# Modulation rows in bursts inside the HGRN scan's slots, and projections ahead of two waits for normed outputs

## The reference, cut to what matters

```
m_lat = (silu(c) @ ada_w[l] + ada_b[l]);  m_ctx = silu(c_ctx) @ ada_w[l] + ada_b[l]
sh1, sc1, g1, sh2, sc2, g2 = split(m, 6)
u = layer_norm(x) * (1 + sc1) + sh1
h = u @ w_in[l]                                  # columns for three mixers
y = concat[rwkv7 scan, differential attention, hgrn2 scan] @ w_out[l]
x = layer_norm(ALPHA * x + g1 * y)
x = layer_norm(ALPHA * x + g2 * peer_ffn(layer_norm(x) * (1 + sc2) + sh2))
```

## Time and profile before

| | us |
|---|---|
| median of 3 runs | 6001.18 (5999.1 to 6006.35) |
| profiled execution | 6002.42 |
| its span, first to last instruction | 6000.6 |
| PE busy | 5152.3 (86%) |
| DVE busy | 3722.8 (62%) |

### The profile page before, as it was taken

How to read it: one execution, slowest core, us unless ns; L and a number is a source line. 1 busy time by engine, 2 the same in 40 slices (tenths; PEclk the granted TensorE clock), 3 DMA queues, 4 the chain that set the end, 5 groups by cost and what they waited for, 6 DMA issues and landing times.

```text
span 6000.6 us, 63022 instructions
## 1 busy us (share of the span) xinstructions
PE 5152.3 (86%) x22127; PEld 3419.4 (57%) x22127; DVE 3722.8 (62%) x8344; ACT 1465.9 (24%) x3650; POOL 1470.7 (25%) x1540
## 2 busy tenths in 40 slices
PE   8899887888776899999999589978798657999997
PEld 3588553667643455555555368845475545666664
DVE  1544371756966797877665455434465786786565
ACT  1111031322566221112111211002222283121111
POOL 0000000000126555545553000000000055344552
PEclk9899988589887999999999789989758757999998
DMA  6000001004358999999997100000002258999996
GB/s 227 21 12 8 21 5 56 1 22 151 124 195 326 366 415 411 400 399 409 401 409 302 62 11 8 8 25 15 35 1 85 105 207 346 416 420 419 416 416 266
DMA packets 294042, 1191.31 MB, mean 199 GB/s; under 512 B 24800, under 2 KB 106976, under 8 KB 208224
## 3 DMA queue, kind: packets, MB, share of 16 engines
q0 software_dynamic: 92160, 671.13, 27.3%
q1 hardware_dynamic: 195808, 460.83, 20.8%
q10 hardware_dynamic: 5760, 55.33, 2.3%
HBM read 1135.81 MB, written 51.38 MB: 198 GB/s over the span
## 4 chain that ended last, share of the span: by engine, by line
PE 62%; DVE 19%; DMA 10%; ACT 4%; issue 2%; POOL 2%; ACTq 0%; DVEq 0%; SPq 0%; POOLq 0%
PE psum L537 62%; DMA arena<-in_ut 6%; DVE arena L1476 3%; DMA arena<-gate_blocks 2%; DVE arena L1631 1%; DVE arena L1822 1%; DVE x_tokens L1476 1%; DVE arena L1897 1%; DMA arena<-in_uv,arena 1%; DVE arena L1485 1%; DMA x_tokens<-in_uv,arena 1%; DVE arena L1629 1%; DVE u_features L1482 1%; DVE y_features L1726 1%; ACT y_features L1169 1%
## 5 line engine op out<-in xcount | busy, mean ns | idle before, releaser
L537 PE MATMUL psum<-arena 128*128 128x64 f32 (+4 forms) x8128 | 1439.3, 352 | 31.2 <-DVE arena L1822 24.2
L537 PE MATMUL psum<-u_features,weight_ring 128*128 128x256 f32 (+2 forms) x4672 | 1351.6, 441 | 31.2 <-ACT arena L1198 17.5
L537 PEld LDWEIGHTS psum<-arena 128*128 128x128 f32 (+1 forms) x8128 | 1032.5, 212 | 399.3 <-issue 309.5
L537 PEld LDWEIGHTS psum<-u_features,weight_ring 128*128 128x128 f32 x4672 | 883.6, 193 | 401.1 <-issue 193.5
L1454 POOL TENSOR_TENSOR arena<-consts 128x1 f32<-128x1 f32 x640 | 335.2, 524 | 1231.3 <-DVE y_features L1726 1098.8
L537 PE MATMUL psum<-u_features,arena 128*128 128x384 f32 (+1 forms) x2048 | 581.5, 438 | 41.3 <-DMA arena<-in_ut 37.2
L537 PE MATMUL psum<-weight_ring,consts 128*128 128x512 f32 x1280 | 570.4, 592 | 2.3 <-DVE consts L1713 1.9
L537 PE MATMUL psum<-arena,y_features 128*128 128x128 f32 (+1 forms) x1632 | 375.3, 387 | 192.1 <-ACT y_features L1171 87.3
L537 PEld LDWEIGHTS psum<-u_features,arena 128*128 128x128 f32 x2048 | 392.3, 192 | 253.7 <-issue 56.3
L1455 POOL DMA_INDIRECT arena<-in_uv,arena x350 | 486.8, 1391 | 99.3 <-POOL arena L1454 94.0
L1087 ACT ACTIVATE arena<-psum 128x512 f32<-128x512 f32 (+5 forms) x388 | 237.6, 612 | 1095.3 <-PE psum L537 864.0
(11 more groups left out here) (208 smaller groups left out, 5361.4 us busy)
## 6 DMA issues: line engine op xcount, KB each, us to landing
weight_ring<-in_ws SPq DMA_DIRECT2D x242, 512.0 KB, 3.6
weight_ring<-in_ut SPq DMA_DIRECT2D x128, 512.0 KB, 10.6
weight_ring<-in_uv SPq DMA_DIRECT2D x128, 512.0 KB, 13.0
arena<-in_ut SPq DMA_DIRECT2D x128, 512.0 KB, 16.2
arena<-in_uv SPq DMA_DIRECT2D x128, 512.0 KB, 10.5
gate_blocks<-arena ACTq DMA_DIRECT2D x20, 2048.0 KB, 7.6
arena<-gate_blocks SPq DMA_DIRECT2D x32, 768.0 KB, 17.8
arena<-gate_blocks SPq DMA_DIRECT2D x32, 512.0 KB, 27.8
```

Of the source, the lines that this page charges most:

```text
L537: return pe.matmul(o, w, x, start=first, stop=last, skip_group_check=True)
```

## The change

Only four chunks of 512 columns (the first 2048, `sh1` and `sc1` of layer 0) stay at the start (`HEAD_ADA`). The other 4096 columns of layer 0 and the first 2048 of layer 1 are computed in layer 0's HGRN scan as 24 chunks of 256 columns, the remaining 4096 of layer 1 in its own scan as 16. `scan_ada` puts a chunk's eight matmuls in front of the level in the slots (n, d) = (1,0), (2,1), (4,0), (5,1), in place of the warm-up multiplication there. `ada_columns` turns the four rows of an iteration in the first slot of the next. ScalarE's copies stand at the iteration's end and behind the next one's first placing. VectorE adds the bias for the later columns in the fifth iteration. The `ada` events leave the opening's list; the rest of that list stays as it was.

The second part: PE projects the last two query/key pieces and the values right after `rwkv g` (which moves to other PSUM banks), and turns `rwkv y` behind the second rotation. After attention it projects four of the six HGRN pieces before it turns `attn y`, and the other two after. ScalarE's copies follow the same order.

```diff
@@ -59,7 +59,9 @@
 ADA, RW, AQK, AV, HF, HT, WO, WQ = 48, 7, 8, 4, 6, 4, 8, 16
-PIECES = [(2 * ADA if l == 0 else 0) + RW + AQK + AV + HF + HT + WO // 2 + WQ * len(QUERIED[l]) for l in range(DEPTH)]
+HEAD_ADA, OWN_ADA = 4, 16
+SCAN_ADA = [24, 16]
+PIECES = [(4 * HEAD_ADA if l == 0 else 0) + 2 * SCAN_ADA[l] + RW + AQK + AV + HF + HT + WO // 2 + WQ * len(QUERIED[l]) for l in range(DEPTH)]
@@ -293,6 +295,9 @@
+        ADA_ROWS = [XT[0:2, 256 * j:256 * (j + 1)] for j in range(4)]
+        ADA_AT, ADA_BANK = ((1, 0), (2, 1), (4, 0), (5, 1)), (3, 4, 0, 7)
+
         def hset(i, d):
@@ -572,6 +572,29 @@
+            def scan_ada(l, i, n, d):
+
+                if (n, d) not in ADA_AT or 4 * i >= SCAN_ADA[l]:
+                    return False
+                j = ADA_AT.index((n, d))
+                if i and n % 2:
+                    pe.wait_ge(*at("scan ada kept", l, 4 * i + j - 4))
+                for k in range(KB):
+                    w = piece_now() if k % 4 else piece_ready()
+                    ins = mm(bank(ADA_BANK[j], 0, 256)[0:2, :], CC[:, 2 * k:2 * k + 2],
+                             w[:, k % 4 * 256:(k % 4 + 1) * 256], k == 0, k == KB - 1)
+                    if k % 4 == 3:
+                        piece_done(ins, *(("scan ada rows", l, 4 * i + j) if k == KB - 1 else ()))
+                return True
+
+            def ada_columns(l, i):
+
+                if 0 <= 4 * i < SCAN_ADA[l]:
+                    pe.wait_ge(*at("scan ada kept", l, 4 * i + 3))
+                    for j in range(8):
+                        ins = mm(bank(0, 2 * j, 2 * j + 2), ADA_ROWS[j // 2][:, j % 2 * P:(j % 2 + 1) * P], ident[0:2, 0:2])
+                    done(ins, "scan ada turned", l, i)
+
             def project(l, what, count, first=0):
@@ -748,8 +771,8 @@
                     pe.wait_ge(*at("cond silu"))
-                    for c in range(ADA // 4 + 1):
-                        if c < ADA // 4:
+                    for c in range(HEAD_ADA + 1):
+                        if c < HEAD_ADA:
                             if c >= 2:
@@ -898,26 +921,26 @@
                 for t in range(NT):
-                    ins = mm(PS[:, t * 256:(t + 1) * 256], lo_[64:128, t * P:(t + 1) * P], SW[64:128, 0:256])
+                    ins = mm(PS[:, 2048 + t * 256:2048 + (t + 1) * 256], lo_[64:128, t * P:(t + 1) * P], SW[64:128, 0:256])
                 done(ins, "rwkv g", l)
-                pe.wait_ge(*at("rwkv y", l))
-                for b in range(2):
-                    for t in tiles(l):
-                        ins = pe.transpose(turned(2 * b, t), RO[:, t * 256 + b * P:t * 256 + (b + 1) * P], ident)
-                done(ins, "rwkv y turned", l)
-                pe.wait_ge(*at("rwkv y features", l))
-
                 project(l, "attn", AQK, NT)
                 pe.wait_ge(*at("attn copied", l, AQK - 1))
+                pe.wait_ge(*at("rwkv y", l))
                 project_tokens("attn", xt, range(NT), "attn v", l)
...
+                    if n == 2:
+                        pe.wait_ge(*at("attn v kept", l))
+                        for b in range(2):
+                            for t in tiles(l):
+                                ins = pe.transpose(turned(2 * b, t), RO[:, t * 256 + b * P:t * 256 + (b + 1) * P], ident)
+                        done(ins, "rwkv y turned", l)
                     if n >= 2:
...
                 pe.wait_ge(*at("rope", l, 7))
-                pe.wait_ge(*at("attn v kept", l))
+                pe.wait_ge(*at("rwkv y features", l))
                 jobs = [(t, h) for t in tiles(l) for h in range(BH)]
@@ -954,14 +977,16 @@
                         done(ins, "attn pv", l, j)
+                project(l, "hgrn", BH)
+                pe.wait_ge(*at("hgrn copied", l, BH - 1))
                 pe.wait_ge(*at("attn y", l))
...
                     done(ins, "attn y turned", l, h)
+                pe.wait_ge(*at("attn y features", l, 1))
+                project(l, "hgrn", HF, BH)
                 pe.wait_ge(*at("attn y features", l, BH - 1))
-
-                project(l, "hgrn", HF)
                 pe.wait_ge(*at("hgrn copied", l, HF - 1))
@@ -972,6 +997,8 @@
                         pe.wait_ge(*at("hgrn scaled", l, i, d))
+                        if i and 4 * (i - 1) < SCAN_ADA[l]:
+                            pe.wait_ge(*at("scan ada kept", l, 4 * (i - 1) + ADA_BANK.index(b0)))
                         for b in range(2):
@@ -984,7 +1011,12 @@
                                 pe.wait_ge(*at("hgrn pairs", l, i, d))
-                            keep_warm(bank(b0 + 2 * (n % 2), 256, 384), 1)
+                            if n + d == 0:
+                                ada_columns(l, i - 1)
+                            if n == 2 and d == 0 and 0 < 4 * i <= SCAN_ADA[l]:
+                                pe.wait_ge(*at("scan ada columns", l, i - 1))
+                            if not scan_ada(l, i, n, d):
+                                keep_warm(bank(b0 + 2 * (n % 2), 256, 384), 1)
                             for h in range(4):
@@ -1009,10 +1041,13 @@
                     pe.wait_ge(*at("hgrn state", l, NT - 1, d))
-                for s in streams:
-                    broadcast(l, "gate1", [16], s, 2 * s)
+                if 4 * NT == SCAN_ADA[l]:
+                    ada_columns(l, NT - 1)
+                    pe.wait_ge(*at("scan ada columns", l, NT - 1))
+                broadcast(l, "gate1", [16], 0, 0)
                 broadcast(l, "mod2", [24, 32], 0, 4)
                 if len(streams) > 1:
+                    broadcast(l, "gate1", [16], 1, 2)
                     pe.wait_ge(*at("gate1 kept", l, 1))
@@ -1040,13 +1075,6 @@
                         key_scores(l, n, c)
-                    if kind == "ada":
-                        if n:
-                            pe.wait_ge(*at("next ada rows kept", n - 1))
-                        if n < ADA // 4:
-                            ada_rows(7, "next ada rows", n)
-                        if n:
-                            ada_turned(6, 384, MRN, "next ada turned", n - 1)
                     if kind == "turn":
@@ -1111,6 +1139,11 @@
                     done(act.activation(q["ta"], q["ta"], ACT.Exp), "rwkv decays", l, i, d)
+
+            def columns_kept(l, i):
+
+                act.wait_ge(*at("scan ada turned", l, i))
+                copy(MCN[:, 16 * i:16 * i + 16], bank(0, 0, 16), "scan ada columns", l, i)
@@ -1283,16 +1316,15 @@
                         copy(q["u"], bank(b0 + 1, 0, 256), "rwkv U kept", l, i, d)
-                act.wait_ge(*at("rwkv y turned", l))
-                lo = 0 if l + 1 < DEPTH else CTX
-                copy(yt(0, lo), pair(0, lo))
-                copy(yt(1, lo), pair(2, lo), "rwkv y features", l)
-
                 for c in range(NT, AQK):
...
                 copy(VA, PS[:, 0:NT * 512], "attn v kept", l)
+                act.wait_ge(*at("rwkv y turned", l))
+                lo = 0 if l + 1 < DEPTH else CTX
+                copy(yt(0, lo), pair(0, lo))
+                copy(yt(1, lo), pair(2, lo), "rwkv y features", l)
                 jobs = [(t, h) for t in ts for h in range(BH)]
@@ -1311,11 +1343,14 @@
                         copy(PT_[(n - 1) % 2][:, 0:keys], PS[:, 2048:2048 + keys], "attn aT", l, n - 1)
+                for c in range(BH):
+                    act.wait_ge(*at("hgrn projected", l, c))
+                    copy(AR[:, c * T:(c + 1) * T], pair(2 * (c % 2)), "hgrn copied", l, c)
                 for h in range(BH):
...
-                for c in range(HF):
+                for c in range(BH, HF):
                     act.wait_ge(*at("hgrn projected", l, c))
@@ -1336,9 +1371,21 @@
                         copy(q["ktm"], bank(b0, 0, 256), "hgrn k kept", l, i, d)
+                    if 0 < 4 * i <= SCAN_ADA[l]:
+                        act.wait_ge(*at("hgrn placed", l, i, 0, 0))
+                        columns_kept(l, i - 1)
                     if i + 1 < NT:
                         hgrn_decays(l, i + 1)
+                    for j in (1, 2, 0, 3) if 4 * i < SCAN_ADA[l] else ():
+                        h, d = 4 * i + j, ADA_BANK[j] // 4
+                        act.wait_ge(*at("scan ada rows", l, h))
+                        act.wait_ge(*at("hgrn placed", l, i, d, LEVELS - (ADA_BANK[j] % 4 == 0)))
+                        if i:
+                            act.wait_ge(*at("scan ada turned", l, i - 1))
+                        copy(ADA_ROWS[j], bank(ADA_BANK[j], 0, 256)[0:2, :], "scan ada kept", l, h)
                 done(act.activation(HS, HG, ACT.Sigmoid), "hgrn g gate", l)
+                if 4 * NT == SCAN_ADA[l]:
+                    columns_kept(l, NT - 1)
                 for s in streams:
@@ -1766,11 +1805,11 @@
                     ts2(LB[:, 12:16], LB[:, 8:12], -1.0, 1.0, ALU.mult, ALU.add)
-                dve.wait_ge(*(at("next ada cols") if l else at("ada turned", ADA // 4 - 1)))
```

(14 more changed lines are left out.)

32 lines of the change are left out of this document (11 added, 21 removed).

## The result

The changed kernel took 5855.85 us (median of 4 runs, 5847.91 to 5858.70) against 6000.78 of the kernel before on the same chip: a ratio of 0.9755, 95% interval [0.9738, 0.9772]. That is 145 us faster; the forecast was 5844, its own range 5820 to 5870 and the whole range 5800 to 5905. The profiled execution took 5856.14 us, span 5854.3.

The account below looks back on a forecast made before the run. PE was taken to bound most stages, waiting only at the norms. Start -63.5, norms -42.3 and -37.9, opening -73.5, second scan +60 sum to -157.2 on 6002.4, so 5844 us; own range 5820 to 5870, whole range 5800 to 5905.

Parts of the forecast that it names:

- Start: Kernel start: eight of twelve modulation chunks go, 7.94 us each, -63.5 us, between -62 and -64.
- Norms: Norms after first scan and after attention, both layers: projections fill PE's idle time, -42.3 and -37.9 us.
- the first norm: Norm after the first scan: PE projects two pieces while idle, -22.1 and -22.0 us before charges, sum -42.3.
- the turns behind the second rotation: Norm after the first scan: turns of its output, mostly beside VectorE's rotary work, charged 1.3 and 0.5 us.
- The second norm: Norm after attention: four of six pieces projected ahead hide it fully, -22.3 and -15.6 us, sum -37.9.
- Opening: Layer 0's gate blocks without modulation chunks: -50 us for 28 blocks, -23.4 for the next 24, sum -73.5.
- Rival 2: Opening of layer 0: fetches or VectorE's routing set 3.3 and 4.2 us a block, total 5865 to 5875; chance 14%.
- Second scan: HGRN scans: 40 chunks added, 37.3 us an iteration, +34 layer 0, +10 layer 1, 16 for dips, total +60.
- the 16 us for dips of the clock: Second scan: 16 us added for the clock falling between an iteration's last burst and the next one's first.
- Rival 1: Second scan: clock falls in every gap, iterations 43 to 48 us, scan +110, total 5895; chance 18%.
- Rival 3: Cheaper second scan without dips, +35, and opening at 2.72 and 3.5 us a block, total 5810; chance 13%.
- Rival 4: Second scan: bursts and everything else at 1.2 GHz, 64 us an iteration, scans +305, total 6090; chance 3%.

Follow-up runs that it names:

- the late burst: The changed kernel with the fourth burst of each iteration in slot (7,1) instead of (5,1), warm-ups kept: 5835.53 us, ratio 0.9702 to the kernel before.
- quarter chunks: The changed kernel with only two of each scan chunk's eight matmuls, warm-ups kept: 5853.39 us, ratio 0.9733 to the kernel before.
- all three edits: The changed kernel with column turn in slot (1,1), fourth burst in (7,1), no warm-up in the HGRN scan: 5778.97 us, ratio 0.9610 to the kernel before.
- turn and last burst late: The changed kernel without warm-ups in iterations with bursts, column turn in slot (1,1), fourth burst in (7,1): 5781.56 us, ratio 0.9620 to the kernel before.
- quarter bursts and no warm-ups: The changed kernel with two of each scan chunk's eight matmuls and no warm-ups in iterations with bursts: 5778.14 us, ratio 0.9607 to the kernel before.

## Why the prediction was right

**Start, right to 0.4 us.** Eight periods of 7.94 us, and nothing late behind them.

**Norms, right, 5 us too small.** The working of the first norm held to a microsecond in both layers. Of the 1.8 us charged in all for the turns behind the second rotation, 0.6 is seen (43.5 gained of the 44.1 ahead of this charge). The second norm gave 23.8 and 18.1 for 22.3 and 15.6. From the last attention turn to the scan it is 23.4 and 16.3; the other 0.4 and 1.8 are attention itself, shorter with the same instructions (in layer 1 at a clock of 0.96 instead of 0.93).

**Opening, right in sum.** The first 28 blocks took 2.91 us each, for 2.86. The next 24 took 4.09 and not the 3.86 of layer 1's blocks, -17.9 instead of -23.4; the remaining blocks gave 6 us that the prediction had not counted. Rival 2 asked for 3.3 and 4.2: the first half of it is refuted, the second half nearly true but worth 5 us.

**Second scan, right in kind, 14 us too cheap.** PE became the bound, the clock rose, and iterations were 41 to 44 us where the prediction put 37.3 plus 1.6 for dips. The term that was too small is the 16 us for dips of the clock. In the 41.0 us iteration PE is busy 38.34 us at 0.92, and by estimate the same work at full clock would be 0.92 x 38.34 = 35.3: three microseconds are lost to the low clock in the best iterations and up to six in the 44.0 one (41.34 against the same 35.3), and not 1.6. The prediction's own working had 4 to 8 us for a dip and charged a fraction of it, with no reason given. Two small terms were off against each other: the eight turns take 1.94 us at full clock and not 1.1 (the 2.16 us row was eight turns already, two records for each, and not sixteen), and four warm-ups less save 1.7 and not 1. Where the dips are was argued rightly, from the last burst to the next iteration's first; the late burst, which changes nothing else, shows it (clock 0.92 to 0.96, 1.5 us less PE time for the same work, 18 us in all). Layer 1 came near its +10 by luck: the last iteration, which has no bursts, ran at full clock in 23.3 us for a forecast of 36.6; its burst iterations were dear like the others. At the low clock it would have added some 14 us (37.1 us for it in the kernel before), and the total would stand near 5870, the upper end of the forecast's own range.

**Rival 1** (clock falls in every gap, 43 to 48 us an iteration) is refuted in its size for the kernel after: one iteration of 44.0 us, the others 40.7 to 42.9, the scans +74 and not +110. Its reason holds for one gap, the one across an iteration's end (0.76 and then 0.70), and fails between the bursts (1.00). The whole rival is what happens with quarter chunks: 0.54 and 44.4. The bursts' length decides between the two. **Rival 3** fails with the dips, and its 2.72 and 3.5 us a block with the 2.91 and 4.09. **Rival 4** needs bursts at 1.2 GHz; thirty of the forty took 3.61 or 3.62 us, the first of each iteration 4.05 to 5.51.

**What the prediction had left out** is what the warm-ups cost. It took the 35.5 us of PE work of an iteration as given, and 11.5 of them were warm-ups; without them an iteration takes 28.7 to 30.4 us at clocks of 0.55 to 0.66. Up to the turns behind them the two scans take 439.6 us before, 513.2 after (+73.6), 371.2 before without warm-ups and 424.1 with all three edits. So the bursts cost 142 us in the form that they have in the kernel after, half of it hidden in a comparison with a padded scan, and 53 us in the best form, for 136 us that they take out of the start and the opening. Set against a scan without warm-ups, the bursts of the kernel after gain nothing. No run has the norm part on the kernel before without its warm-ups. By estimate, 5941.7 less the 80 to 85 us of the norms, it would take some 5860, about as long as the kernel after, without moving a single modulation chunk. That rival stands untested.

The Trainium skill, page "TensorE: Matmul & The Clock Gate", section "HAM oscillation — how this bites in real kernels", has the clock fall at PE's pauses. These runs disagree with it as the only cause: the granted clock was 0.54 with PE busy 42.88 of 44.30 us (quarter chunks, longest pause 1.42) and 0.75 with PE busy 24.99 of 34.10. The prediction gave the measurement the say over this rule, and with it the 16 us for dips; the rule would have left them out and missed the scans by 30 us.

## What to carry to other kernels

Before work is moved into a stage that PE bounds at half clock, read how much of PE's time there is padding: one warm-up per slot cost 16 x 0.72 us an iteration, bought little clock, and its removal was worth 74 us by itself. Take it out first and judge the move against that kernel. Then place the long multiplications so that the largest gap between two of them shrinks, across an iteration's end above all: moving one burst was worth 18 to 25 us at the same work. Judge each part by landmarks and by the granted clock of each iteration, since iterations with the same instructions took 23.3 or 39.2 us (with warm-ups), and 15.9 or 23.3 (without), by the clock that they happened to get.

## What the runs showed of the hardware

- A busy PE doesn't always keep its clock here: with small matmuls, warm-ups and quarter bursts it was granted 0.54 while busy 97% of an iteration. With four whole bursts of sixteen passes of 256 columns it got 0.92 (busy 94%), with the warm-ups taken out and turn and last burst late 1.00 or 0.86 (busy 91 and 93%), with quarter bursts and no warm-ups 0.75 (busy 73%). The same small matmuls and warm-ups without bursts were granted 0.56 in one kernel's last iteration and 1.00 in another's. What the chip goes by can't be read from these rows.
- The bursts that hold the clock have only two stationary columns (128*2), so filling the array isn't needed for it. Shortening each burst to a quarter brought the clock from 0.92 to 0.54; other shapes were not tried.
- Sixteen passes of 256 columns (eight matmuls, two records each) took 3.61 us, about half of the 7.03 for 512 columns, at the full granted clock.
